# A two-block network on one core: the root of each norm taken as a power on GpSimd, narrower causal scores, a re-ordered start and end of layers

## The reference

```python
def rms_norm(x, g):
    xf = x.astype(jnp.float32)
    y = xf * lax.rsqrt(jnp.mean(xf * xf, axis=-1, keepdims=True) + EPS)
    return (y * g.astype(jnp.float32)).astype(x.dtype)

# first block
h = rms_norm(x, g_mix)                      # then q, k, v, z, xbc, dt = split(h @ w_in)
attn = dilated_attention(q, k, v, ...)      # 16 heads of 64, q and k normed per head, causal window
attn = rms_norm(attn, g_attn_out)
ssm  = ssd_mixer(z, xbc, dt, ...)           # state-space scan, normed in 4 groups
x = x + concat([attn, ssm]) @ w_out
x = x + cross_attention(rms_norm(x, g_cross), rms_norm(mem, g_mem), ...)   # 4 heads, q and k normed
x = x + square(relu(rms_norm(x, g_mlp) @ w_up)) @ w_down
# second block
n = rms_norm(h, attn_norm)                  # c_q, c_kv, k_r, x_r, y_r, ga, gr = split(n @ w_in)
y_attn = mla_branch(...)                    # 16 heads of 192, causal; norms q_norm and kv_norm inside
y_rnn  = rglru_branch(...)
h = h + (sigmoid(ga) * y_attn + sigmoid(gr) * y_rnn) @ w_out
h = h + peer_ffn(rms_norm(h, ffn_norm))     # per token 8 x 16 expert rows of u and of v, gathered
h = h + sigmoid(rms_norm(h, ple_norm) @ w_ple_gate) * (p @ w_ple_proj)
return rms_norm(h, final_norm)
```

## Time and profile before

| | us |
|---|---|
| median of 3 runs | 3889.14 |
| lowest and highest run | 3883.0, 3893.53 |
| the profiled execution | 3886.61 |
| its span, first to last instruction | 3884.6 |
| PE busy | 3305.3 (85%) |
| DVE busy | 2470.6 (64%) |
| ACT busy | 1428.7 (37%) |
| POOL busy | 847.1 (22%) |

### The profile page before, as it was taken

How to read it: one execution, slowest core, us unless ns; L and a number is a source line. 1 busy time by engine, 2 the same in 40 slices (tenths; PEclk the granted TensorE clock), 3 DMA queues, 4 the chain that set the end, 5 groups by cost and what they waited for, 6 DMA issues and landing times.

```text
span 3884.6 us, 53098 instructions
## 1 busy us (share of the span) xinstructions
PE 3305.3 (85%) x21008; PEld 2742.1 (71%) x21008; DVE 2470.6 (64%) x3257; ACT 1428.7 (37%) x2042; POOL 847.1 (22%) x623
## 2 busy tenths in 40 slices
PE   8988998999999999999999996766666666666688
PEld 8977887999999999999998996732222223222248
DVE  6567865654455556875546666977777776555556
ACT  6555555553345444564445452221000111000124
POOL 2000011000000100000000011255665565565522
PEclk9998999999999999999999997888888888888899
DMA  6423253555556565555552455899999999999964
GB/s 231 148 98 109 96 160 110 162 185 187 183 179 190 176 200 174 163 180 184 166 179 96 157 185 213 315 355 422 421 422 422 422 422 420 421 421 421 421 260 140
DMA packets 188023, 952.98 MB, mean 245 GB/s; under 512 B 20992, under 2 KB 20992, under 8 KB 121984
## 3 DMA queue, kind: packets, MB, share of 16 engines
q0 software_dynamic: 73728, 536.90, 33.6%
q1 hardware_dynamic: 114048, 412.70, 33.0%
HBM read 947.42 MB, written 2.10 MB: 244 GB/s over the span
## 4 chain that ended last, share of the span: by engine, by line
PE 58%; DMA 18%; DVE 13%; ACT 4%; POOL 4%; issue 2%; DVEq 0%; ACTq 0%; POOLq 0%; SPq 0%
PE ps L524 58%; DMA BIG<-in_peer_v,CS 6%; DMA HLF<-in_peer_v,CS 6%; DVE HL L1748 3%; DMA HF<-in_peer_v,CS 3%; DVE BIG L1752 2%; POOL HLF L506 2%; POOL BIG L506 2%; DMA BIG<-in_peer_u,CS 2%; DVE BIG L2390 1%; DMA HLF<-in_peer_u,CS 1%; DVE BIG L1748 1%; ACT BIG L1115 1%; ACT HL L1121 1%; PE ps L528 1%
## 5 line engine op out<-in xcount | busy, mean ns | idle before, releaser
L524 PE MATMUL ps<-HS,HL 128*128 128x256 f32 x10128 | 1344.8, 288 | 36.0 <-DVE HL L1748 29.9
L524 PEld LDWEIGHTS ps<-HS,HL 128*128 128x128 f32 x10128 | 1291.8, 196 | 47.5 <-DVE HL L1748 34.7
L1748 DVE TENSOR_TENSOR HL<-RAW,HL 128x1024 fp32r<-128x1024 f32 (+1 forms) x772 | 954.6, 1237 | 237.4 <-ACT HL L1121 174.1
L1121 ACT CAST HL<-RAW 128x1024 fp32r<-128x1024 f32 (+1 forms) x772 | 805.4, 1043 | 502.1 <-PE ps L524 454.4
L524 PE MATMUL ps<-BIGR,HL 128*128 128x256 f32 x6720 | 893.3, 284 | 24.2 <-DVE HL L1748 14.8
L524 PEld LDWEIGHTS ps<-BIGR,HL 128*128 128x128 f32 x6720 | 849.0, 192 | 32.2 <-issue 14.8
L524 PE MATMUL ps<-BIG,HF 128*128 128x512 f32 (+1 forms) x760 | 398.8, 675 | 191.2 <-DMA BIG<-in_peer_v,CS 168.1
L524 PE MATMUL ps<-HLF,HF 128*128 128x512 f32 x656 | 342.5, 674 | 154.2 <-DMA HLF<-in_peer_v,CS 140.6
L524 PEld LDWEIGHTS ps<-BIG,HF 128*128 128x128 f32 (+1 forms) x760 | 161.3, 222 | 423.3 <-issue 386.0
L473 POOL COPY NSUM<-TMP 128x256 f32<-128x256 f32 x6 | 3.3, 553 | 1957.6 <-ACT TMP L1117 1957.6
L2390 DVE CUSTOM_DVE_ANT_0 BIG<-BIG 128x2048 f32<-128x2048 f32 x133 | 305.0, 2293 | 167.3 <-DMA BIG<-in_peer_u,CS 158.1
(11 more groups left out here) (194 smaller groups left out, 2235.3 us busy)
## 6 DMA issues: line engine op xcount, KB each, us to landing
RAW<-in_w_up SPq DMA_DIRECT2D x128, 512.0 KB, 4.0
RAW<-in_w_down SPq DMA_DIRECT2D x128, 512.0 KB, 4.2
RAW<-in_w_out SPq DMA_DIRECT2D x64, 512.0 KB, 4.3
RAW<-in_w_qk SPq DMA_DIRECT2D x32, 512.0 KB, 3.4
RAW<-in_w_xbc SPq DMA_DIRECT2D x32, 512.0 KB, 3.5
RAW<-in_w_xr SPq DMA_DIRECT2D x32, 512.0 KB, 3.5
RAW<-in_w_yr SPq DMA_DIRECT2D x32, 512.0 KB, 3.8
RAW<-in_w_gr SPq DMA_DIRECT2D x32, 512.0 KB, 4.4
```

The costliest lines, as they stand in the source:

```text
L524: return e.matmul(o, l, r, start=start, stop=stop, skip_group_check=True)
L1121: s.done(e.copy(o, i), sig)
L1748: v.done(e.tensor_tensor(o, a, b, op), sig)
```

## The change

1. The root. DVE takes mean and epsilon from PSUM (`mean`, one `TENSOR_SCALAR`), POOL raises the result to the power -1/2 (`root`, one `tensor_tensor` with `ALU.pow`), and DVE waits for it (`rooted`, on the new counter `s_root`). ACT's Sqrt and DVE's reciprocal are gone for all 15 norms, for the 4 groups of q and k and for the 4 cross heads. POOL's roots stand in one line with its additions and gathers; that of ple_norm is behind all gathers.
2. The first query tile meets only the first 128 keys (`CAUSAL`), in scores, mask, maximum and exp, for the 16 dilated and the 16 mla heads.
3. PE's `norm_end` of g_cross, g_mlp, attn_norm and ffn_norm comes behind the next layer's first unit. DVE makes the low half of that layer's unit 2 ahead of the mean and of unit 3 ahead of the wait for the root.
4. `by_vector`: of the last 16 rows of `v` DVE takes the 8 with odd k, before 4 of them.
5. `w2_pg` joins `LATE`; PE does two half sums behind its first unit, and DVE's order ahead of it is another.
6. ACT multiplies `X` by the final gain chunk by chunk during `w2_pg`; at the end DVE has four products of 128x1024 with `RS` in place of 16.

```diff
-LATE = ("w_ck", "w_out", "w2_ao")
+LATE = ("w_ck", "w_out", "w2_ao", "w2_pg")
+CAUSAL = ((0, 128), (128, 256))
         def by_vector(g):
-            return g[0] == "u" or g[2] % 4 == 3
+            return g[0] == "u" or g[2] % 4 == 3 or (g[1] == 15 and g[2] % 2 == 1)
 # POOL
+            def root(x, name, n=0, sig=None):
+                g.wait_ge(*((s_nfree, NORM[name] + 1) if sig is None else sig))
+                g.prev()
+                g.done(e.tensor_tensor(x, x, con("minus_half").to_broadcast([128, x.shape[-1]]), ALU.pow), (s_root, ROOT[name] + n + 1))
...
+            root(RX, "g_mix")
+            for G in range(4):
+                root(SS, "qk", G, (s_gsum, G + 1))
+            root(RS[:, 1, :], "attn")
...
 # PE, in dense
                         p.then_inc(s_mm, 1)
+                        if norm is not None and u == L.unit0:
+                            norm()
...
-                    for i in range(2):
-                        p = mm(b[:, i * T:i * T + T], QK[lo:lo + 64, c, i * 128:i * 128 + 128], QK[lo:lo + 64, 8 + c, :],
+                    for i, (at, w) in enumerate(CAUSAL):
+                        p = mm(b[:, at:at + w], QK[lo:lo + 64, c, i * 128:i * 128 + 128], QK[lo:lo + 64, 8 + c, 0:w],
...
-            norm_end("g_cross")
-            dense(L["w_cq"], normed("g_cross"), evac_cq, g_cr)
+            dense(L["w_cq"], normed("g_cross"), evac_cq, g_cr, lambda: norm_end("g_cross"))
 # ACT
-                act(dst, norm_bank[:, 0:T], ACT.Sqrt, (s_nfree, NORM[name] + n + 1), bias=con("eps"), scale=1.0 / div)
+                act(OUT[:, c, :], X[:, c, :], ACT.Identity, (s_xg, c + 1), scale=vec("final_norm", c))
 # DVE
+            def mean(dst, src, div, sig):
+                ts(dst, src, 1.0 / div, EPS, ALU.mult, ALU.add, sig)
-            def norm_end(name):
+            def norm_end(name, L=None):
                 normed_low(name, 15)
-                v.wait_ge(s_nfree, NORM[name] + 1)
-                recip(RX, RX, (s_rx, RXN[name]))
+                if L is not None:
+                    low(L.unit0 + 2)
+                v.wait_ge(s_nsum, ADDED[name] + 1)
+                norm_mean(RX, name, 2048)
+                if L is not None:
+                    low(L.unit0 + 3)
+                rooted(name)
...
-            recip(RS[:, 0, :], RS[:, 0, :])
-            for c in range(16):
-                stt(OUT[:, c, :], X[:, c, :], vec("final_norm", c), RS[:, 0, :], ALU.mult, ALU.mult,
+            norm_mean(RS[:, 0, :], "final", 2048)
+            rooted("final")
+            v.wait_ge(s_xg, 16)
+            for i in range(4):
+                tt(o, o, RS[:, 0, :].unsqueeze(1).to_broadcast([128, 4, T]), ALU.mult, (s_pout, i + 1))
```

More of the change, by code:

```diff
@@ L121 @@
 HALF = counted([("attn", 3), ("ssm0", 2), ("ssm1", 2), ("ssm2", 2), ("ssm3", 2)])
-RXN = {"mem": 1, "g_mix": 2, "g_cross": 3, "g_mlp": 4, "attn_norm": 5, "ffn_norm": 6, "ple_norm": 7}
+ROOT = counted([("mem", 1), ("g_mix", 1), ("qk", 4), ("attn", 1), ("ssm0", 1), ("ssm1", 1), ("ssm2", 1), ("ssm3", 1), ("g_cross", 1),
+                ("cross", 4), ("g_mlp", 1), ("attn_norm", 1), ("q_norm", 1), ("kv_norm", 1), ("ffn_norm", 1), ("ple_norm", 1), ("final", 1)])
 NORMED = counted([(n, 16) for n in ("g_mix", "g_cross", "g_mlp", "attn_norm", "ffn_norm", "ple_norm")])
+CAUSAL = ((0, 128), (128, 256))
 class Engine:
@@ L492, in gpsimd @@
             g.wait_ge(s_sq, SQ["mem"] + 1)
+            g.wait_ge(s_con, 16)
+            root(KEEP[:, 0, :], "mem")
             square_sums("g_mix", 1)
-            for name in ("g_cross", "g_mlp", "attn_norm", "ffn_norm"):
-                square_sums(name, 1)
+            root(RX, "g_mix")
[3 more added lines that the diff above has]
+            for i in range(4):
+                root(RS[:, i % 2, :], f"ssm{i}")
+            square_sums("g_cross", 1)
+            root(RX, "g_cross")
+            for h in range(4):
+                root(den(h)[:, 6:8], "cross", h, (s_cmean, h + 1))
+            for name in ("g_mlp", "attn_norm"):
+                square_sums(name, 1)
+                root(RX, name)
+            root(RS[:, 1, :], "q_norm")
+            root(RS[:, 0, :], "kv_norm")
+            square_sums("ffn_norm", 1)
+            root(RX, "ffn_norm")
             e.wait_ge(s_turn, TURN["rows"] + 8)
@@ L1187, in first @@
                     yield
-                norm_end("g_mix")
                 yield
@@ L1918, in attn @@
             def attn(h):
-                yield from softmax_head("attn", h, AP_[h % 4], 4, 1.0, con("mask"), True, 3)
+                yield from softmax_head("attn", h, AP_[h % 4], 4, 1.0, 3)
             def log1p_exp(x, m, y, z, p, n):
@@ L2296, in mla @@
             def mla(h):
-                yield from softmax_head("mla", h, MP[h % 3], 3, 192.0 ** -0.5, con("mask"), True)
+                yield from softmax_head("mla", h, MP[h % 3], 3, 192.0 ** -0.5)
             v.wait_ge(s_mask, 16)
@@ L2475, in vector, with normed_lows @@
             drain(g_ex)
-            for b in range(4):
-                joined(1, b)
-            pg = L["w2_pg"].unit0
-            for j in range(5):
-                if j < 4:
-                    added(1, j)
-                if j in (0, 4):
-                    low(pg + j // 4)
-                if j:
-                    for c in range(4 * j - 4, 4 * j):
-                        normed_low("ple_norm", c)
-            v.wait_ge(s_nfree, NORM["ple_norm"] + 1)
-            recip(RX, RX, (s_rx, RXN["ple_norm"]))
+            pg = L["w2_pg"].unit0
+            def normed_lows(j):
+                for c in range(4 * j, 4 * j + 4):
+                    normed_low("ple_norm", c)
+            for b in range(3):
+                joined(1, b)
+            added(1, 0)
+            joined(1, 3)
+            added(1, 1)
+            low(pg)
+            normed_lows(0)
+            added(1, 2)
+            normed_lows(1)
+            low(pg + 1)
+            added(1, 3)
+            low(pg + 2)
+            normed_lows(2)
+            normed_lows(3)
+            low(pg + 3)
+            v.wait_ge(s_sq, SQ["ple_norm"] + 8)
+            mean(RX, PS[7][:, 0:T], 2048, (s_nfree, NORM["ple_norm"] + 1))
+            rooted("ple_norm")
             def evac_pg(c):
```

218 lines of the change are left out of this document (96 added, 122 removed).

## The result

The changed kernel takes 4436.08 us (median of 4 runs, 4435.5 to 4438.89) against 3887.93 us (4 runs, 3883.0 to 3893.53): a ratio of 1.1411, 95% interval 1.1391 to 1.1431. It is 548 us slower. The prediction, 3852 us with a range of 3825 to 3905, was wrong in size and in sign. What came is rival 1, the dear power, at a price far outside the bounds.

What follows compares the result with a forecast made beforehand. PE was taken to bound most of the kernel and the DMA gathers the stretch from 2394 to 3743 us. At a power of 3.0 us the terms summed to 35.0 us off 3886.6, giving 3852 us, range 3825 to 3905.

Steps and rivals of the forecast that it cites:

- rival 1: Power on POOL costs 8 us or more, DVE's low halves queue behind `rooted`, run slower, 3901 to 3922 us; chance 0.16.
- The price of the power: p, POOL's time for a power of 128x256 values: taken as 3.0 us, between 0.72 and 9.8.
- The exposure: Gain lost per us of the power's price: 8.5 us, 11.5 above 5.8; attn, ssm, q and kv norms half exposed.
- cover: At g_mlp the first result is taken out 9 us behind the sums, hiding a power of up to about 5.8 us.
- groups of q and k and cross heads: Table loads and small roots leave ACT, so waits of DVE and PE go: gains of 8 and 4.6 us.
- layer boundaries: Sums behind the next layer's first unit: gains 2.4 at g_cross, 2.9 at g_mlp, 2.2 each at attn_norm and ffn_norm.
- narrower scores: Shorter score matmuls on PE: gain 8.5 us, 6.8 from the mla heads and 1.7 from the dilated heads.
- last rows: Last rows of `v` end sooner with DVE taking more of them: gain 3.7 us, or 0 if DVE's rows came late.
- `w2_pg`: PE's first matmul there starts sooner with DVE's new order ahead of it: gain 2.5 us, from 0.8 to 4.2.
- Final products: At the end, 16 products of 8.30 us become four taking 4.9 us: gain 3.4 us.
- dearer roots: Power slower than root and reciprocal: -1 at start, -2 for attn and ssm norms, -1 for q and kv, -1.3 at end.
- DVE's waits for POOL sum to more than about 35 us: Sign, in the profile after the change, that the forecast is wrong.

Runs made afterwards that it cites:

- small_powers: sqrt_back with the power on POOL only for the four groups of q and k and the four cross heads: 3852.7 us, ratio 0.9917.
- power_16: Changed kernel; for the 15 large roots DVE writes 1.0 for the mean and POOL's power takes the first 16 columns only: 3854.56 us, ratio 0.9920.
- sqrt_back: Changed kernel with only the root put back, square root on ACT and reciprocal on DVE: 3866.65 us, ratio 0.9952.
- sums_ahead: sqrt_back with the sums of g_cross, g_mlp, attn_norm and ffn_norm ahead of the next layer's first unit again: 3873.37 us, ratio 0.9969.
- pg_in_order: sqrt_back with w2_pg, and the work of PE, ACT and DVE ahead of it, in the former order: 3869.9 us, ratio 0.9962.
- end_as_before: sqrt_back with 16 products on DVE at the end and none on ACT ahead, as before: 3868.25 us, ratio 0.9952.

## Why the prediction was wrong

**The price of the power** is the step that failed: "Below ... p = 0.72 ... Above ... 2 x 4.2 x 1.175 = 9.8. I take 3.0". It is 41.1: 14 times the value taken and 4.2 times the upper bound. The bound was built on an analogy: a function was taken to cost as many times an addition on POOL as a reciprocal costs on DVE. But POOL's shortest addition is 0.72/256 = 0.0028 us per column, the power 0.159, 57 times that. Nothing in the trace of before shows a function of this kind on POOL, and no row excluded such a factor. The upper end then was no bound but a second estimate, and the range, which ends at 3905, did not even reach what that end gives, 3922, though the prediction says that it keeps both ends.

The Trainium skill, page "GPSIMD Engine Reference", section 3.1, was cited for a factor of about 2 in elementwise work and for 12 cycles per element of branching, an estimated 2.6 us. The factor holds for additions alone. For the power no run here bears either figure out; its advice to leave elementwise work off GpSimd would have been right for the fifteen wide tiles, and wrong for the eight small ones, as small_powers shows.

**The exposure** was mis-sized as well: 8.5 us per us of p, 11.5 above 5.8, where the runs show 15 to 16. "Half exposed" for the seven norms of attn, ssm, q and kv was wrong, since DVE waits 41.2 us in each of seven, and PE with it. The "cover" of g_mlp did not help either. In power_16 PE runs on there without a stop; in the changed kernel it works off three units, about 10 us, and then stands for 35.63 us. The stage still grew by 38.2 us from power_16 to the changed kernel, which is all of what the price grew by, 41.1 - 2.9. The difference is in the work behind the stall, which begins at half the clock, 23 matmuls in the first 5 us against 44 in the next:

```profile
1040.00:1045.00 5.00, 4.94 (x23) 4.94 (x24) 3.66 (x6) 2.40 (x4) 0.00 (x0) 0.51 0.68 209
1045.00:1050.00 5.00, 5.00 (x44) 5.00 (x44) 1.71 (x3) 2.22 (x4) 0.00 (x0) 1.00 0.67 212
```

Rival 1 named the mechanism rightly, low halves queued behind `rooted`, and got a chance of 0.16.

**The sum at p = 3.0** was right as a whole: 35 forecast, 3887.0 - 3854.6 = 32.4 measured in power_16. That it came so near is in part luck, since terms that were too high by some 13 us stand against others too low by some 11. Its terms, against the runs:

- groups of q and k and cross heads, 8 + 4.6: small_powers gives 14 for both. In the profiles the stage up to g_cross is 5.2 us shorter than in sqrt_back (3.5 to 7.2 against before and the versions with one part undone), and that of the cross heads 9.1 (6.7 to 11.4): the first term was too high, the second too low. The idle time that went at the cross heads, 5.1, is near the 4.6; the other 3.9 is the clock, which the prediction did not count there.
- layer boundaries, 9.7: 6.7 in sums_ahead. PE still waits for the sums of g_mlp behind the first unit, 2.99 us, as the row at 993.58 shows; the first unit's 2.88 us are the whole gain there, as forecast.
- narrower scores, 8.5: 1.3 by whole runs, and 0 to 2.6 in the mla stage where 6.8 were expected. What failed in this term is "in a stretch where PE has next to no idle time, so all of it counts": PE waits 1.9 us longer for ACT's copy at the last heads, and some 9 us of work behind that run at half the clock.
- last rows, 3.7: 3.6 in their stage (3.1 against pg_in_order and end_as_before). `w2_pg`, 2.5 (0.8 to 4.2): 3.3. Final products, 3.4: 3.1.
- dearer roots at the start, -1, in the seven chains of attn, ssm, q and kv, -3, and at the end, -1.3: power_16 and small_powers differ in the fifteen wide roots alone, 2.9 us on POOL against square root and reciprocal on ACT and DVE. Both gain 32.4 us over the kernel before, so at that price these losses are not there, but for 0.7 us in the last stage (12.4 against 11.7).

What was predicted to be seen: POOL's rows gave p at once; `joined` starts right behind the last row and `w2_pg` 8.7 us behind it in `sqrt_back`, where 11 to 12 were expected; "DVE's waits for POOL sum to more than about 35 us" was the sign for wrong, and they sum to over 600.

## What to carry to other kernels

An operation that no trace shows has no upper bound from an analogy: measure it alone before it goes into fifteen critical places, or let the range and the chances say that its price is unknown. When an engine is given a new function, ask what is queued behind the wait on the engine that uses the result; here a POOL instruction stopped PE through DVE's queue. A slow function can still pay where the tile is a few columns wide and a step of other work lies before its use, as small_powers shows; and a part that is worth a few us is read in its own stage, not in the whole run.

## What the runs showed of the hardware

- POOL's power (`tensor_tensor` with `pow`, float32) takes some 0.35 us and 0.159 us per column (41.12 us for 256 columns, 20.72 for 128, 10.52 for 64, 2.89 for 16), 41.1 us for 256 columns of 16, 32, 64 or 128 partitions alike, and 20.72 and 20.78 us for 128 columns with the exponents -0.5 and 1.
- At one place a wait of PE of 3.26 us was followed by a stretch at a granted clock of 0.50, 10.2 us long, in ten profiles; behind a wait of 1.37 to 1.74 us at the same place the clock stayed at 1.00 in three and was at 0.50 for 3.4 us in one. Narrowing work on PE brought the longer wait and the lower clock about.
- At the cross heads, with table loads and roots on ACT, the granted clock was 0.87 to 0.92, with the roots on POOL 0.97 and 0.98: 3.9 of the 9.1 us gained there against `sqrt_back` are the same matmuls taking less time.
